# Expert weights loaded as two consecutive rows per partition, and used in pairs of chunks

## What is computed

```python
def ec_moe(h, w_r, w_gate, w_up, w_down):       # 16 experts, F = 1024
    cap = EC_CAPACITY * n // N_EXPERTS           # 32 tokens for each expert
    aff = jax.nn.softmax(jnp.einsum("bnd,de->bne", h, w_r), axis=-1)
    gates, idx = lax.top_k(jnp.swapaxes(aff, 1, 2), cap)
    xs = h[bidx, idx]
    hid = jax.nn.silu(jnp.einsum("becd,edf->becf", xs, w_gate)) * jnp.einsum("becd,edf->becf", xs, w_up)
    ys = jnp.einsum("becf,efd->becd", hid, w_down) * gates[..., None]
    return jnp.zeros_like(h).at[bidx, idx].add(ys)
```

## Time and profile before

| | |
|---|---|
| time, median of 3 runs | 1809.87 us (1807.76 to 1810.55) |
| span of the profiled execution | 1797.7 us |
| median less span | 12.2 us |
| PE busy | 1329.2 us, 74% |
| moved by DMA | 561.76 MB, mean 312 GB/s |
| issued expert loads | 192 of 2048 KB each |

### The profile page before, as it was taken

The page is one execution under the profiler, slowest core; times in us unless marked ns, Lnnn a source line. Parts: engine busy times, 40 slices in busy tenths (PEclk is TensorE's granted clock), DMA queues, the critical chain, the costliest instruction groups (busy, mean ns, idle before and its releaser), DMA issues.

```text
span 1797.7 us, 18131 instructions
## 1 busy us (share of the span) xinstructions
PE 1329.2 (74%) x7744; PEld 741.4 (41%) x7744; DVE 490.5 (27%) x706; ACT 348.7 (19%) x515; POOL 150.9 (8%) x142
## 2 busy tenths in 40 slices
PE   4988867565587596579775655655556998899999
PEld 1653551121141141169521201212113876779997
DVE  1259450010110000056510100101004644446553
ACT  1111420000010000033300000000003533544442
POOL 1034000000000000010000000000003033440000
PEclk8999969888887798889888988988888988999999
DMA  9898839999999999995479999999999540434530
GB/s 341 355 379 340 322 132 365 409 410 409 404 361 386 406 408 409 407 389 199 152 297 409 410 409 410 410 410 410 410 410 360 208 141 31 159 138 159 187 124 24
DMA packets 160187, 561.76 MB, mean 312 GB/s; under 512 B 9548, under 2 KB 10948, under 8 KB 153470
## 3 DMA queue, kind: packets, MB, share of 16 engines
q1 hardware_dynamic: 155224, 551.83, 78.7%
q0 software_dynamic: 2208, 8.36, 1.2%
q10 hardware_dynamic: 2694, 0.68, 0.2%
HBM read 557.69 MB, written 3.16 MB: 312 GB/s over the span
## 4 chain that ended last, share of the span: by engine, by line
PE 33%; DMA 28%; SPq 4%; DVE 3%; ACT 2%; issue 1%; POOL 0%; DVEq 0%; ACTq 0%; POOLq 0%
PE ps L1821 21%; DMA ring<-in_moe_w_down 12%; DMA ring<-in_moe_w_up 12%; SPq L457 4%; DMA ring<-in_moe_w_gate 4%; PE ps L2062 4%; PE ps L1806 3%; PE ps L2070 1%; DMA ring<-in_w_in 1%; PE ps L2267 0%; PE ps L2095 0%; PE ps L2255 0%; PE ps L2257 0%; PE ps L1868 0%; ACT ring_parts L579 0%
## 5 line engine op out<-in xcount | busy, mean ns | idle before, releaser
L2062 PE MATMUL ps<-ring,scratch 128*32 128x512 f32 x3072 | 472.6, 753 | 321.8 <-DMA ring<-in_moe_w_up 134.8
L2062 PEld LDWEIGHTS ps<-ring,scratch 128*32 128x32 f32 x3072 | 97.2, 124 | 671.3 <-DMA ring<-in_moe_w_up 205.7
L1821 PE MATMUL ps<-ring_parts,scratch_parts 128*128 128x512 f32 x656 | 185.3, 401 | 5.1 <-DVE scratch_parts L1353 1.4
L1821 PE MATMUL ps<-scratch_parts,ring_parts 128*128 128x256 f32 x704 | 146.0, 282 | 0.0
L1821 PEld LDWEIGHTS ps<-ring_parts,scratch_parts 128*128 128x128 f32 x656 | 122.3, 188 | 35.7 <-issue 5.0
L579 ACT ACTIVATE ring_parts<-ring 128x2048 fp32r<-128x2048 f32 x56 | 106.1, 1920 | 93.7 <-PE ps L1821 87.4
L1821 PEld LDWEIGHTS ps<-scratch_parts,ring_parts 128*128 128x128 f32 x704 | 116.2, 191 | 0.3
L423 DVE TENSOR_TENSOR ring_parts<-ring,ring_parts 128x2048 fp32r<-128x2048 f32 x44 | 100.7, 2289 | 53.4 <-ACT ring_parts L579 52.1
L1431 DVE TENSOR_TENSOR scratch<-ps,gate_bc 128x512 f32<-128x512 f32 x16 | 10.3, 686 | 306.5 <-PE ps L2062 306.5
L1423 DVE TENSOR_TENSOR scratch<-scratch,ps 128x1024 f32<-128x1024 f32 x8 | 9.8, 1221 | 298.0 <-PE ps L2062 298.0
L1821 PE MATMUL ps<-xT_parts,ring_parts 128*128 128x256 f32 x288 | 80.9, 281 | 1.3 <-DVE xT_parts L1130 1.3
(11 more groups left out here) (375 smaller groups left out, 1584.0 us busy)
## 6 DMA issues: line engine op xcount, KB each, us to landing
ring<-in_moe_w_gate SPq DMA_DIRECT2D x64, 2048.0 KB, 23.4
ring<-in_moe_w_up SPq DMA_DIRECT2D x64, 2048.0 KB, 23.7
ring<-in_moe_w_down SPq DMA_DIRECT2D x64, 2048.0 KB, 23.9
ring<-in_ada_w SPq DMA_DIRECT2D x24, 2048.0 KB, 12.2
ring<-in_mlp_w SPq DMA_DIRECT2D x16, 2048.0 KB, 8.5
ring<-in_sc_w_in SPq DMA_DIRECT2D x6, 2048.0 KB, 21.0
ring<-in_w_in SPq DMA_DIRECT2D x6, 2048.0 KB, 18.0
ring<-in_xattn_wkv SPq DMA_DIRECT2D x4, 2048.0 KB, 24.4
```

Of the source, the lines that this page charges most:

```text
L1821: last = mm(out, lhs[x], rhs[y], start=start and n == 0, stop=stop and n == 2)
L2062: last = mm(ps[32 * j:32 * j + 32, banks[half], :], src[:, k, CAP * j:CAP * (j + 1)], w[:, j, 512 * half:512 * half + 512], start=(k == 0) ...
```

## The change

The row dimension of each expert matrix is cut in another way. Before, it was `(k p)`: chunk k held rows 128k + p. Now it is `(k p j)` with j = 0, 1: in step k partition p holds the two consecutive rows 256k + 2p and 256k + 2p + 1, 8 KB that lie together in HBM. A slot of 16 KB then holds two experts, not four, so a step of all four experts takes two chunks, and PE waits for both before it uses either and gives both back at once (`RUN` = 2, `STEPS` = 4). The contraction index on each partition must match: the gather, the transposes of the hidden rows, of the normalized rows and of the modulation rows read every second column (`run_slice`), and the router weights and `norm2_g` are loaded in the new order. `norm2_g` gets a small buffer of its own and two transposes of 8 rows at the start.

```diff
+RUN = 2
+STEPS = KD // RUN
...
+        grow2 = gate_bc[0:2 * STEPS, 0:P * RUN]
...
+        def run_order(v):
+            return v.rearrange("p (k i j) -> p k j i", i=P, j=RUN)
+        def run_slice(v, k):
+            return run_order(v)[:, k // RUN, k % RUN, :]
...
             def experts(loop):
-                gate = a["moe_w_gate"][l].rearrange("(g e) (k p) f -> g k p e f", e=EG, k=KD)
+                gate = a["moe_w_gate"][l].rearrange("(g q e) (k p j) f -> g k q p e (j f)", g=GROUPS, q=RUN, p=P, j=RUN)
...
                     for c in range(PER_GROUP):
                         w, k = (gate, up, down)[c // KD], c % KD
                         sp.wait_ge(sem("chunks_used"), PER_GROUP * g + (base + c - SLOTS + 1))
-                        sp.dma_start(slot4(base + c), w[g, k])\
+                        sp.dma_start(ring[:, slot_of(base + c), :].rearrange("p (e f) -> p e f", e=EG // RUN), w[g, k // RUN, k % RUN])\
...
-                act.dma_start(wr[:, l], a["moe_w_r"][l].rearrange("(k p) e -> p k e", k=KD)).then_inc(sem("params_in"), 16)
+                act.dma_start(wr[:, l].rearrange("p (k j) e -> p k j e", j=RUN), a["moe_w_r"][l].rearrange("(k p j) e -> p k j e", p=P, j=RUN)).then_inc(sem("params_in"), 16)
...
+                    src = run_slice(flat(mrow[:, g % 3]), b) if g % 3 else mrow[:, g % 3, b, :]
...
+                        cols = run_slice(src[:, t, :], k) if name in ("moe0", "moe1") else src[:, t, P * k:P * (k + 1)]
...
                     def product(c0, banks, src, second=None):
-                        for k in range(KD):
-                            w = chunk(c0 + k)
-                            if second and k == KD // 2:
-                                pe.wait_ge(sem(second), n + 1)
-                            for half in range(2):
-                                for j in range(EG):
-                                    last = mm(ps[32 * j:32 * j + 32, banks[half], :], src[:, k, CAP * j:CAP * (j + 1)],
-                                              w[:, j, 512 * half:512 * half + 512], start=(k == 0), stop=(k == KD - 1))
-                            used(last)
+                        for step in range(STEPS):
+                            w = [chunk(c0 + RUN * step + q) for q in range(RUN)]
+                            for k in range(RUN * step, RUN * step + RUN):
+                                if second and k == KD // 2:
+                                    pe.wait_ge(sem(second), n + 1)
+                                for half in range(2):
+                                    for j in range(EG):
+                                        col = F * (k % RUN) + 512 * half
+                                        last = mm(ps[32 * j:32 * j + 32, banks[half], :], src[:, k, CAP * j:CAP * (j + 1)],
+                                                  w[j * RUN // EG][:, j % (EG // RUN), col:col + 512],
+                                                  start=(k == 0), stop=(k == KD - 1))
+                            last.then_inc(sem("chunks_used"), RUN)
...
-                             last = mm(ps[:, 6 + k // 4, P * (k % 4):P * (k % 4 + 1)], rows[:, t, P * k:P * (k + 1)],
+                             last = mm(ps[:, 6 + k // 4, P * (k % 4):P * (k % 4 + 1)], run_slice(rows[:, t, :], k),
...
-                        last = nc.tensor.transpose(ps[:, 6 + k // 4, P * (k % 4):P * (k % 4 + 1)], hid[:, P * k:P * (k + 1)],
-                                                   ident)
+                        last = nc.tensor.transpose(ps[:, 6 + k // 4, P * (k % 4):P * (k % 4 + 1)], run_slice(hid, k), ident)
```

More of the change, by code:

```diff
@@ L338, in build @@
         SCALE = {"x": 0, "ctx": 1, "moe0": 2, "mix1": 3, "moe1": 4}
-        GAIN = {"mix2": 4, "mem": 5, "xattn": 6, "mlp": 7}
+        GAIN = {"mix2": 2, "mem": 3, "xattn": 4, "mlp": 5}
         def affine(name):
@@ L364, in build @@
         SC_SPLITS = EV_SPLITS + 16
-        GAINS = (8 + SCK) * KD
-        cw1 = gcol[:, 8:8 + SCK, :].rearrange("p j c -> p c j")
+        GAINS = (6 + SCK) * KD
+        NORM2 = 6 + SCK
+        cw1 = gcol[:, 6:6 + SCK, :].rearrange("p j c -> p c j")
         PARAMS = 10
@@ L449, in experts @@
                 l, g0, g1, base = loop
-                gate = a["moe_w_gate"][l].rearrange("(g e) (k p) f -> g k p e f", e=EG, k=KD)
-                up = a["moe_w_up"][l].rearrange("(g e) (k p) f -> g k p e f", e=EG, k=KD)
-                down = a["moe_w_down"][l].rearrange("(g e) (k p) d -> g k p e d", e=EG, p=P)
+                gate = a["moe_w_gate"][l].rearrange("(g q e) (k p j) f -> g k q p e (j f)", g=GROUPS, q=RUN, p=P, j=RUN)
+                up = a["moe_w_up"][l].rearrange("(g q e) (k p j) f -> g k q p e (j f)", g=GROUPS, q=RUN, p=P, j=RUN)
+                down = a["moe_w_down"][l].rearrange("(g q e) (k p j) d -> g k q p e (j d)", g=GROUPS, q=RUN, p=P, j=RUN)
                 with sp.Fori(g0, g1) as g:
@@ L464, in _ @@
             first = 0
-            for g in (a["norm1_g"], a["norm2_g"], a["norm_mix_g_2"].unsqueeze(0), a["norm_mem_g_2"].unsqueeze(0),
+            for g in (a["norm1_g"], a["norm_mix_g_2"].unsqueeze(0), a["norm_mem_g_2"].unsqueeze(0),
                       a["norm_xattn_g_2"].unsqueeze(0), a["norm_mlp_g_2"].unsqueeze(0), a["sc_conv_w"][0]):
@@ L469, in _ @@
                 first += n
+            sp.dma_start(grow2, a["norm2_g"].rearrange("l (k c) -> (l k) c", k=STEPS)).then_inc(sem("gains_in"), 16)
             sp.wait_ge(sem("cleared"), 2)
@@ L1173, in mod_cols @@
                 else:
-                    last = scale(("moe0", "moe1")[g // 3], 0, 2 + g // 3)
+                    last = scale(("moe0", "moe1")[g // 3], 0, NORM2 + g // 3)
                 last.then_inc(sem("mod_cols"), 1)
@@ L1206, in _ @@
             dve.wait_ge(sem("gains_ps"), 1)
-            nc.vector.tensor_copy(flat(gcol[:, :, :]), ps[:, 1, 0:GAINS]).then_inc(sem("gain_cols"), 1)
+            nc.vector.tensor_copy(flat(gcol[:, :, :]), ps[:, 1, 0:GAINS + 2 * KD]).then_inc(sem("gain_cols"), 1)
             normed("x", h, rows)
@@ L1782, in ada_columns @@
                 for b in range(4):
-                    last = nc.tensor.transpose(ps[:, bank, P * b:P * (b + 1)], mrow[:, g % 3, b, :], ident)
+                    src = run_slice(flat(mrow[:, g % 3]), b) if g % 3 else mrow[:, g % 3, b, :]
+                    last = nc.tensor.transpose(ps[:, bank, P * b:P * (b + 1)], src, ident)
                 last.then_inc(sem("mod_T"), 1)
@@ L1876, in _ @@
             pe.wait_ge(sem("gains_in"), 7 * 16)
-            nc.tensor.transpose(ps[:, 1, 0:GAINS], grow[0:GAINS, :], ident[0:GAINS, 0:GAINS]).then_inc(sem("gains_ps"), 1)
+            nc.tensor.transpose(ps[:, 1, 0:GAINS], grow[0:GAINS, :], ident[0:GAINS, 0:GAINS])
+            for j in range(RUN):
+                last = nc.tensor.transpose(ps[:, 1, GAINS:GAINS + 2 * KD].rearrange("p (r j) -> p j r", j=RUN)[:, j, :],
+                                           grow2.rearrange("r (i j) -> r j i", j=RUN)[:, j, :],
+                                           ident[0:2 * STEPS, 0:2 * STEPS])
+            last.then_inc(sem("gains_ps"), 1)
             pe.wait_ge(sem("sil"), 1)
@@ L2051, in chunk @@
                         pe.wait_ge(sem(f"slot{i % SLOTS}_loaded"), 16 * (PER_GROUP // SLOTS) * g + 16 * (i // SLOTS + 1))
-                        return slot4(i)
+                        return ring[:, slot_of(i), :].rearrange("p (e f) -> p e f", e=EG // RUN)
                     def product(c0, banks, src, second=None):
-                        for k in range(KD):
-                            w = chunk(c0 + k)
-                            if second and k == KD // 2:
-                                pe.wait_ge(sem(second), n + 1)
-                            for half in range(2):
-                                for j in range(EG):
-                                    last = mm(ps[32 * j:32 * j + 32, banks[half], :], src[:, k, CAP * j:CAP * (j + 1)],
-                                              w[:, j, 512 * half:512 * half + 512], start=(k == 0), stop=(k == KD - 1))
-                            used(last)
+                        for step in range(STEPS):
[10 more added lines that the diff above has]
+                            last.then_inc(sem("chunks_used"), RUN)
                     pe.wait_ge(sem("mo_h"), 4 * n + 1)
```

2 lines of the change are left out of this document (1 added, 1 removed).

## The result

The changed kernel takes 1795.88 us, median of 15 runs (1785.43 to 1799.29), against 1806.96 us for the kernel before, also of 15 (1794.69 to 1810.55). The ratio is 0.9942, with a 95% interval from 0.9921 to 0.9963. In a second comparison of 12 runs against 29 it was 0.9941, 0.9915 to 0.9967. So the change makes the kernel 0.6% faster, some 11 us; forecast were 1786.5 us and a gain of 23.4. Of the 15 runs of the kernel before 7 lie under 1801 us, the others near 1808, so that its median mixes two kinds of run; the experiments part them.

The account below looks back on a forecast made before the run. The prediction took the full DMA queue to bound the expert stretches. Its terms, -33.4 + 5.2 + 3.8 + 1.0 = -23.4 us, gave a span of 1774.3 us and, with 12.2 us to the median, 1786.5 us; range 1776 to 1803.

Parts of the forecast that it names:

- 168 chunks are load time, and all scale with the rate: Expert loops: 168 of 192 chunks cost their load time, 860 us of the 1797.7.
- The rate: Expert loads: 8 KB rows raise 410 to 426.2 GB/s, 0.199 us less a chunk, 33.4 us less in all.
- Restarts: Three places where the stream stands: the ninth chunk waits for two used chunks, 1.74 us each, 5.2 us more.
- Ends of loops: First and third loop: two chunks stand behind the last landing, not one; 1.9 us more each, 3.8 together.
- End of the second loop: Ahead of the third loop: the stream's 8 us in hand are used up; 1 us of gap, 0 to 2.
- The sum: Whole kernel: -33.4 + 5.2 + 3.8 + 1.0 = -23.4 us, giving 1786.5 us.
- The stream holds inside the loops, with 6 chunks ahead: Inside loops: 6 chunks, 29.5 us of loading, cover PE's longest absence of 20.4 us, so no cost.
- The strided reads: PE's gathers and transposes reading every second column: taken as nothing; upper end 18.2 us and some 4 for router transposes.
- the 12.2 us between span and median are taken to stay: Whole kernel: 12.2 us added to the forecast span of 1774.3 us to give 1786.5 us.
- Rival 2: Expert loads: only part of the rate step comes with the row; 415 GB/s, 1810 us, no difference; chance 0.06.
- Rivals 1 and 3: 1: the gather pays double, 1805 to 1809 us, chance 0.08; 3: expert rows stay at 410 GB/s, 1819 to 1820, 0.07.
- Rival 4: Expert products: PE at its slow pace throughout; a 7.1 us pair fits in 9.84, 3.6 us more at ends; no chance given.

Follow-up runs that it names:

- `before_again`: The kernel before, unchanged, run again: 1804.32 us, ratio to itself 0.9974.
- the 16 KB kernel: The changed kernel with RUN = 4: four consecutive rows, 16 KB per partition, one expert in a slot, chunks used four at a time; 1820.89 us, ratio 1.0081.

## Why the prediction was right in kind and off in size

- **168 chunks are load time, and all scale with the rate.** Right. The kernel with the 8 KB rows alone is 23.9 us faster, by the times and by the table, and 168 x 0.150 is 25.2.
- **The rate.** The term was too large: 33.4 forecast, 25.2 by the rate of 422 GB/s (4.970 us a chunk; PE's pairs in layer 1 start at 971.85 and 991.72, two pairs in 19.87 us, which is 4.968). The failing step was to take the windows of `ada_w` as the rate of a long stream. They are stretches of 8 to 12 us of a stream that stops and starts between them. Windows of 8 us inside the expert stream after read from 417 to 428, where the long ones read 422; with 4 KB rows they had stayed within 408 to 412. The prediction's own argument, that 410 was the same in 16 us and in 446, thus held for 4 KB alone. In a long full stream the 8 KB row costs 310.6 ns an engine, not 307.5. The straight line was right: 84.7, 159.8, 310.6 and, from the 16 KB kernel at 427, 614 ns lie on 9 ns a row and 37.8 ns for each KB within 1 ns. The Trainium skill's section "Why small descriptors are slow" in "DMA: Bandwidth & Descriptors" would have 1.1% here, an estimate from its 3 cycles per packet. The trace has 2.9%, and the measurement decides.
- **Restarts.** Right: 3.70 us after the first product at all three (270.78, 536.12 and 907.99 less 267.08, 532.42 and 904.29), 1.7 more than before.
- **Ends of loops.** Too small: 1.9 us forecast for each, but the pair takes 5.1 to 6.6 us behind the last landing. The profile before happened to show two ends at the slow pace, 3.50 and 3.23 us; that of `before_again` has 1.92 at the third, as the second loop has in both. Against a mean of 2.7 the pair adds some 3 us. All its costs together were sized about right: the pair alone measured 12.7 us by the times and 10.9 by the table, where 10.0 were forecast.
- **End of the second loop.** Right: 1 us of gap forecast. The changed profile has 311 and 379 GB/s from 668 to 676 us, 1.5 us of loading missed.
- **The sum.** With 422 GB/s in place of 426.2 the same working gives -25.2 + 10.0 = -15.2. The slower cluster has -14.7, of which 12.8 lie behind the first product. The two parts alone, -23.9 and +12.7 by the times, add up to -11.2, which is as near as clusters of 5 and 8 runs come.
- **The stream holds inside the loops, with 6 chunks ahead.** Right: 422 GB/s over all of layer 1, no gap.
- **The strided reads.** Right to take almost nothing: 0.2 us for a gather, 2 us at most for all. The rule of the Trainium skill ("SBUF — State Buffer", "Door 1", on 16-byte lines), by which float32 can be read at a step of two for free, agrees with the gather's loads, 192 and 197 ns. For the transposes of the hidden rows it is not free: their weight loads take 209 ns in place of 141. The matmul record of such a transpose goes from 273 to 283 ns, and inside the loops the load of the weight chunks covers it.
- **Not seen: the clock of the second block.** The step "the 12.2 us between span and median are taken to stay" was wrong. Outside the span are 1.9 us (1798.06 less 1796.2). The rest was that the profile shown was one of the faster cluster and the median one of the slower. The sum was thus made on a faster run, and the same 13.5 us came back in the profile after, where they hide nearly the whole gain. The forecast difference was not touched by it, but the comparison of the two profiles was.
- **Rivals.** Rival 2 named the term that was off: 12 of the 16 GB/s came with the row, not all. Its number is farther away than the forecast's own: it had the gain per chunk at 0.06 us, the forecast at 0.199, and 0.150 was measured. Rivals 1 and 3 are refuted by the gathers and by the windows. Rival 4, the slower pace, is seen in part: pairs run at a mix of both paces and still fit.
- **The range.** 1795.88 us lies in it, 9.4 us above the forecast: 8.2 us of that are the rate. The rest is small by luck: 2 us of the reads and some 3 us by which the first product came earlier, neither in the sum, nearly cancel. It is luck too that the three runs that the sum started from and 26 of 27 runs of the changed kernel all fell into the slower cluster.

## What to carry to other kernels

Longer rows speed up a stream that fills the DMA queue, but in these traces the price of a row is only about 9 ns an engine: 3% from 4 to 8 KB, 1% from 8 to 16. Read the rate from a stream as long as the one it is to stand for. If the longer row makes the unit of waiting larger, count every place where the stream stops or ends, because there each unit is paid in full; at four chunks of eight slots those places cost more than the rate gives. A mixed form, long rows in the stream and short units at its edges, kept most of both: -17.3 us, of -23.9 for the rows alone.

Before two profiles are compared, check that they are of the same kind: the distance from one event, here the fall of the clock, to the end should be equal where the code is.

## What the runs showed of the hardware that was not expected

- PE stays at 0.50 of its clock for 30.8 or 61.5 us in the same code, with PE busy in 57 of the 61.5 us, and the runs of one kernel fall into clusters 13.4 us apart. Four extra matmuls in the middle raised the clock for 6.8 us only.
- Rows of 4 KB that lie 8 KB apart stream at 406 to 408 GB/s, those that lie together at 410.
- The weight load of a 128x128 float32 transpose of every second column takes 209 ns in place of 141, that of a matmul 197 in place of 192.
